# Hybrid decoder block: in the stick-breaking stage k's second half is scaled and split one slot later and q's first mean squares run behind their slot's projection part; in norm 1 GpSimd's weight splits wait for the last scaling

## The reference

```
h = rms_norm(x, norm1_g); proj = h @ w_in          # q, k, v of 16 heads of 64, GLA inputs, gates
q, k = rms_norm per head of sb_q, sb_k             # stick-breaking attention (A)
z = q k^T / 8;  mask: key < query
log_not = log_sigmoid(-z) where mask
w = exp(log_sigmoid(z) + sum of log_not over the keys between);  o_sb = w @ v
o_gla = gated linear attention (B)                 # runs before A in this kernel
x = x + (sigmoid(g1) * (o_sb @ W1) + sigmoid(g2) * (o_gla @ W2)) @ w_out
x = x + ffn(rms_norm(x))
```

## Time and profile before

| what | value |
|---|---|
| median of 3 runs | 2198.25 us (2191.25 to 2201.38) |
| the profiled execution | 2198.49 us, span 2196.8 us |
| TensorE matmul busy | 2099.5 us (96% of the span) |
| TensorE weight loads busy | 1711.6 us (78%) |
| VectorE busy | 1282.8 us (58%) |
| GpSimd busy | 931.0 us (42%) |
| ScalarE busy | 761.5 us (35%) |
| mean granted clock of TensorE | 0.982 |

### The profile page before, as it was taken

How to read it: one execution, slowest core, us unless ns; L and a number is a source line. 1 busy time by engine, 2 the same in 40 slices (tenths; PEclk the granted TensorE clock), 3 DMA queues, 4 the chain that set the end, 5 groups by cost and what they waited for, 6 DMA issues and landing times. The chain is left out here.

```text
span 2196.8 us, 30123 instructions
## 1 busy us (share of the span) xinstructions
PE 2099.5 (96%) x10120; PEld 1711.6 (78%) x10120; DVE 1282.8 (58%) x1863; ACT 761.5 (35%) x1329; POOL 931.0 (42%) x817
## 2 busy tenths in 40 slices
PE   5999999999999999999998799997999999999999
PEld 4788888887777777777776688885788888888887
DVE  5559686852468568568566656458544444444444
ACT  3333343311345445446445300005333322222232
POOL 3323231322434434434435233335755555555552
PEclk7999999999999999999999899998999999999999
DMA  3211121222431431431541822211211111101112
GB/s 114 52 29 51 36 55 25 59 70 71 98 93 33 104 93 33 105 83 39 106 87 47 307 86 76 86 48 48 77 58 57 57 39 56 53 25 56 57 57 77
DMA packets 137778, 153.86 MB, mean 70 GB/s; under 512 B 7665, under 2 KB 112113, under 8 KB 137729
## 3 DMA queue, kind: packets, MB, share of 16 engines
q1 hardware_dynamic: 136000, 150.07, 25.0%
q10 hardware_dynamic: 1728, 3.15, 0.4%
HBM read 107.06 MB, written 20.97 MB: 58 GB/s over the span
## 5 line engine op out<-in xcount | busy, mean ns | idle before, releaser
L123 POOL TENSOR_TENSOR w_hi<-w_raw,w_ones 128x64 fp32r<-128x64 f32 x88 | 38.2, 434 | 689.7 <-PE gla_g L149 308.2
L498 POOL TENSOR_TENSOR sb_rows<-sb_beta,sb_rest 128x128 f32<-128x128 f32 (+7 forms) x128 | 154.4, 1207 | 234.3 <-DVE sb_rest L864 207.5
L127 POOL TENSOR_TENSOR w_lo<-w_raw,w_hi 128x512 fp32r<-128x512 f32 x176 | 239.8, 1383 | 7.3
L864 DVE TENSOR_TENSOR_SCAN sb_rest<-sb_rest 128x128 f32<-128x128 f32 (+7 forms) x128 | 211.0, 1649 | 36.9 <-ACT sb_beta L714 36.9
L870 DVE TENSOR_TENSOR sb_wt_lo<-sb_t,sb_wt_hi 128x512 fp32r<-128x512 f32 (+2 forms) x186 | 103.4, 556 | 137.8 <-ACT sb_wt_hi L722 135.5
L149 PE MATMUL sb_g<-h_hi,w_hi 128*128 128x512 f32 x544 | 157.0, 415 | 2.0 <-DVEq L767 1.9
L149 PE MATMUL sb_g<-h_lo,w_hi 128*128 128x512 f32 x544 | 152.7, 405 | 0.0
L722 ACT CAST sb_wt_hi<-sb_t 128x512 fp32r<-128x512 f32 (+2 forms) x186 | 89.7, 483 | 176.7 <-PE sb_t L600 175.6
L149 PE MATMUL sb_g<-h_hi,w_lo 128*128 128x512 f32 x544 | 150.7, 401 | 0.0
L149 PE MATMUL gla_g<-h_hi,w_hi 128*128 128x512 f32 x480 | 130.2, 407 | 3.2 <-DVEq L1321 3.2
L1873 POOL TENSOR_TENSOR ff_w_lo<-ff_raw_g,ff_w_hi 128x512 fp32r<-128x512 f32 x66 | 85.6, 1297 | 102.8 <-ACT ff_w_hi L1983 102.8
(11 more groups left out here) (333 smaller groups left out, 5058.0 us busy)
## 6 DMA issues: line engine op xcount, KB each, us to landing
w_raw<-w_in SPq DMA_DIRECT2D x64, 512.0 KB, 8.1
ff_raw_g<-w_ffn_gate SPq DMA_DIRECT2D x11, 1024.0 KB, 5.5
ff_raw_u<-w_ffn_up SPq DMA_DIRECT2D x11, 1024.0 KB, 5.9
ff_raw_d<-w_ffn_down SPq DMA_DIRECT2D x11, 1024.0 KB, 4.9
sb_qs<-sb_q_st SPq DMA_DIRECT2D x32, 256.0 KB, 5.1
sb_kh<-sb_k_st SPq DMA_DIRECT2D x32, 256.0 KB, 5.0
sb_kl<-sb_k_st SPq DMA_DIRECT2D x32, 256.0 KB, 5.0
mp_sig<-gates_t SPq DMA_DIRECT2D x16, 512.0 KB, 4.3
```

The costliest lines, as they stand in the source:

```text
L123: self.nc.gpsimd.tensor_tensor(hi[:, 0:64], raw[:, 0:64], self.ones[:], ALU.mult)
L127: ins = self.nc.gpsimd.tensor_tensor(lo[:, at], raw[:, at], hi[:, at], ALU.subtract)
L498: nc.gpsimd.tensor_tensor(rows[tb // 4][:, tb % 4, 0:width], beta[:, n % 2, 0:width], rest[:, n % 2, 1:width + 1], ALU.mult).then_inc(row_ ...
L864: nc.vector.tensor_tensor_scan(back, back, back, 1.0, ALU.mult, ALU.bypass).then_inc(scanned, 1)
```

## The change

In the stick-breaking stage, for the seven iterations that prepare a pair: TensorE's mean squares of q's first half (slot 13) and its spread of k's first half (slot 14) go behind the fill of their slot. On VectorE `copy_ms` goes behind `k_root` and `repeat_k_rs` in slot 13; `scale_k` of the second half goes from slot 18 to 19, and `high_k` and `low_k` of the second half from slot 19 to 20. In norm 1 GpSimd waits, before its two splits, until all eight tiles are scaled.

```diff
@@ norm_transposed, GpSimd
                 W.prime_pool(pool)
+                pool.wait_ge(xg_ready, TT)
                 for n in range(len(following)):
                     W.split(pool, 0, n)
@@ slots
-MS_AFTER = [10, 17]
+MS_AFTER = [10, 13, 17]
-SPREAD_AFTER = 18
+SPREAD_AFTER = [14, 18]
+SCALE_SLOT = [14, 19]
+HIGH_K_SLOT = [15, 20]
@@ stick_breaking, TensorE
-                        if not last and s in SPREAD_SLOT and s != SPREAD_AFTER:
+                        if not last and s in SPREAD_SLOT and s not in SPREAD_AFTER:
...
-                        if not last and s == SPREAD_AFTER:
+                        if not last and s in SPREAD_AFTER:
@@ stick_breaking, ScalarE
-                            if s in (15, 19):
-                                high_k(it + 1, (s - 15) // 4, g_uses(it) + 4)
+                            if s in HIGH_K_SLOT:
+                                high_k(it + 1, HIGH_K_SLOT.index(s), g_uses(it) + 4)
@@ stick_breaking, VectorE
-                            if s in MS_SLOT:
-                                i = MS_SLOT.index(s)
-                                copy_ms(i // 2, i % 2, g_uses(it) + 2 * (i // 2) + 1)
                             if s in (11, 12, 13):
                                 k_root(it + 1, g_uses(it) + 1, s - 11)
                             if s == 13:
                                 repeat_k_rs()
-                            if s in SPREAD_SLOT:
-                                scale_k(SPREAD_SLOT.index(s), g_uses(it) + 4)
-                            if s in (15, 19):
-                                low_k(it + 1, (s - 15) // 4)
+                            if s in MS_SLOT:
+                                i = MS_SLOT.index(s)
+                                copy_ms(i // 2, i % 2, g_uses(it) + 2 * (i // 2) + 1)
+                            if s in SCALE_SLOT:
+                                scale_k(SCALE_SLOT.index(s), g_uses(it) + 4)
+                            if s in HIGH_K_SLOT:
+                                low_k(it + 1, HIGH_K_SLOT.index(s))
```

## The result

The changed kernel's median is 2181.64 us (2178.98 to 2189.30, 13 runs), against 2193.95 us (2190.34 to 2201.38, 13 runs) for the kernel before. The ratio is 0.995, 95% interval 0.9941 to 0.9959: 11 us faster (9 to 13), right at the 0.5% that the prediction drew as its line. The first three runs of before had 2198.25 as their median, 4 us above that of all thirteen, and the profiled execution took 2198.49.

The account below looks back on a forecast made before the run. TensorE, busy nearly throughout, was taken as the bound. Stick-breaking 9.3, norm 1 0.9 and the clock 1.5 summed to 11.7 us off the profiled 2198.49: 2187 us, own range 2181 to 2191, over all cases 2180 to 2197.

Parts of the forecast that it names:

- Slots 13 and 14: TensorE in slots 13 and 14: putting the fills first saves 0.58 and 0.21, together 0.79 us an iteration.
- The chain to slot 20: From TensorE's transposes in slot 15 to the longest scan in slot 18: follows TensorE, so the whole 0.79 us comes through.
- What is late next, `scale_k` of the first half: VectorE before `wt_lo` of slot 15: `scale_k` shifts by less than 0.1 us, hidden, with 0.99 us of idle remaining.
- Slots 18 to 20: With `wt_lo` ahead of `scale_k` and `sum_o` sooner, slot 20's weighing starts earlier: another 0.54 us an iteration.
- SyncE's queue: Stacking DMAs and weight load start about 0.6 us later, but 1.7 us of slack is left: nothing lost.
- slack 3.6: Before the change, the weight load lands at 897.7 and GpSimd wants it at 901.33: 3.6 us to spare.
- Rival (c): `low_k` is pushed behind a whole GpSimd split, delaying the weight load: 15 us lost against 9.3 gained, 2202 us; chance 0.06.
- Norm 1: GpSimd's wait leaves VectorE's scalings undisturbed and the block ends sooner: 0.9 us gained, bounds 1.0 either way.
- the last group starts at 22.30 beside GpSimd's splits: VectorE in norm 1: undisturbed, its scalings and two low tiles would end at 30.7, gaining VectorE 3.8 us.
- The clock: Slots 13 and 14: the drop to granted 0.78 in one iteration of seven goes away, saving 1.5 us.
- The sum: Whole kernel: 9.3 + 0.9 + 1.5 = 11.7 us off the profiled 2198.49, giving 2187 us.

## Why the prediction was right

**Slots 13 and 14: right.** Forecast 0.79 an iteration; alone 0.79 (82.33 to 81.54). The chain to slot 20 followed as said.

**What is late next, `scale_k` of the first half: right.** It started at 849.33 in the changed kernel, after 0.30 idle for its spread, with 0.85 idle left before `wt_lo` of slot 15 (forecast 0.99).

**Slots 18 to 20: right, 0.54 forecast, 0.66 measured.** Against the start of slot 18's scan the weighing came 0.57 sooner (6.13 instead of 6.70), as worked out. The missing 0.1 is a cost that the sum left out: the first weighing behind the wait took 0.33 to its neighbour (877.40 to 877.73), the undisturbed one 0.23. A wait need not be the reason, which stays open: behind the short mean squares, with no wait, it took 0.32 too (845.03 to 845.35 in the changed kernel). With 1.49 an iteration instead of 1.33 the term is 10.4 us for seven, not 9.3.

**SyncE's queue: wrong, "nothing" forecast, about 0.9 us lost.** In the fourth iteration, from which it was worked out, the forecast left 1.7 of slack and 2.7 were there, since `low_k` ran clear of GpSimd in 0.73 us and was done at 867.8. It was GpSimd's L124 that took 1.44 instead of 1.00 beside it. Which of the two is stretched goes by who starts: the Trainium skill says so in "SBUF — State Buffer", in the section on the two sides of SBUF (whichever starts first gets the pair of ports for the whole instruction), and here the trace agrees, `low_k` at 867.09 ahead of L124 at 867.24 (GpSimd's short L123, from 866.95 to 867.27, had started ahead of `low_k` and shows no effect on it). The step that failed is "slack 3.6", one iteration's margin taken for all seven: in the kernel before it was 1.7 to 4.1 in six of them, and in the seventh the load was late already. The changed kernel kept 0.5 to 3.1 in the six, so nothing was lost there, and in the seventh the load came 1.2 later still. Rival (c) was to decide from 2.3 us of delay at the landing; that too holds for the fourth iteration only, and one slot more ate most of the gain.

**Norm 1: wrong.** The step "the last group starts at 22.30 beside GpSimd's splits", with 0.9 us gained, took one execution's landing of the weights for a fixed one. The splits themselves ran unstretched beside the low parts (3.82 and 3.85 us), as forecast, and the block started the next stage at 16.7 behind the last root. But without the wait it did so at 16.4 on average, anywhere from 14.7 to 17.6. The gain of 0.9 is not there; a small loss is not shown either.

**The clock: right in size, 1.5 forecast, 1.4 counted.** That the new order of slots 13 and 14 keeps the clock up is shown by 0 of 63 against 5 of 35; that it is the fill ahead of the mean squares, as the prediction had it, is not separated from the gap that went with it.

**The sum.** 10.4 - 0.9 + 1.4 = 10.9 us, with nothing for norm 1, against 11 (9 to 13) from the ratio and 12.3 from the two medians. That the forecast of 11.7 came so near is in part luck: 0.9 for norm 1 and nothing for the queue were each about 0.9 too favourable, and slots 18 to 20 gave 1.1 more than forecast. The forecast 2187 lies 5 us above the measured 2181.6 mainly since it was counted down from a profile at 2198.5, while the kernel before takes 2194.

The parts alone, by the same sum: slots 18 to 20 7 x 0.66 - 0.7 = 3.9 us, against 3.5 (1 to 6) from the ratio; slots 13 and 14 7 x 0.79 + 1.4 - 0.2 = 6.7, against 4.4 (2.4 to 6.4), which stays open. What blurs such totals is seen at the start of the stick-breaking stage: from its first product to the first mask product it took 53.1 us in the profiles without a fall of the clock, 54.5 to 54.7 with 3.4 us at half clock and 60.9 with 17 us, in versions that do the same work there. What decides between them was not pinned down.

## What to carry to other kernels

When an operation of the in-order engine waits for a bank, put behind it in the queue whatever has its inputs already; then look what the moved work frees later, because here `scale_k` in slot 14 was left with 0.85 us of cover and the weight load in one iteration with 0.5. Before you book a gain in a start-up stage, see a second profile: a landing that shifts by one microsecond moved the result from 17.6 to 14.7. Before you book slack of a load, read it in every iteration and in the last one above all: the same load took 6.8 us in one and 13.2 in another, and behind the first half microsecond each one of lateness cost one.

## What was not expected of the hardware

A fall of the granted clock to half inside an otherwise busy stage came only behind one place, two waits of 0.5 us with eight products of two columns behind them, and in one of seven passes; with the second wait gone and a fill of 1.5 us ahead of the short products, it did not come. And the time that the 512 KB load takes to land goes by the iteration and hardly by the version: over all fourteen profiles 6.6 to 7.6 us in the second, 6.9 to 7.6 in the fourth, 8.8 to 9.7 in the sixth and 12.7 to 14.2 in the seventh, whether the next store was issued 1.3 or 5.6 us behind it. Why is open.
